# A two-block transformer kernel on one core: idle matmuls, parameter loads, factor rows and the differential maps' scaling

## The chip, the core and the metric

The kernel runs on one core of a Trainium2 chip. The metric is device time in microseconds of one execution. Five engines work beside each other, each on its own list of instructions: TensorE (PE in the profile; its weight loads are PEld), VectorE (DVE), ScalarE (ACT), GpSimd (POOL) and SyncE (SP), which here only issues transfers from memory. They wait for each other by semaphores, which the kernel sets by hand.

## What is computed

Two transformer blocks, one after the other, on 256 tokens of width 1024, all in float32:

```python
def first_block(x, ...):
    h = rmsnorm(x, norm_mix_pre)                    # mixer: q, k, v, forget logits, conv, gates
    m = mixer(h, w_in, b_f, conv_w, w_branch, w_out)
    x = x + rmsnorm(m, norm_mix_post)
    f = swiglu(rmsnorm(x, norm_ffn_pre), w_gate_up, w_down)
    return x + rmsnorm(f, norm_ffn_post)

def second_block(x, mem, ...):
    x = x + 0.5 * swiglu_2(rms_norm(x, norm_ffn1), ffn1_w1, ffn1_w3, ffn1_w2)
    x = x + hybrid_mixer(rms_norm(x, norm_mix), ...)     # retention and differential attention
    x = x + memory_attention(rms_norm(x, norm_mem_q), rms_norm(mem, norm_mem_kv), ...)
    x = x + 0.5 * swiglu_2(rms_norm(x, norm_ffn2), ffn2_w1, ffn2_w3, ffn2_w2)
    return rms_norm(x, norm_out)

def diff_attention(q, k, v, lam):                        # inside hybrid_mixer, 4 heads
    ...
        p = jax.nn.softmax(sc, axis=-1)
        a = p[:, :, 0] - lam * p[:, :, 1]
        return jnp.einsum('bhqk,bkhe->bqhe', a.astype(v.dtype), v)
# and on its output: rms_norm(do, diff_norm) * (1.0 - lam_init)
```

The last line matters here: whatever factor a row of `a` carries is divided out again by the root mean square that follows, but for the `EPS` under the root.

## The kernel before

Every weight matrix is cut into chunks of 1 MB (161 of them, numbered in the order of their use). SP loads a chunk into one of three places of `stage`; ACT rounds it to `w_hi` (`hi(c)`, L1002), DVE takes the difference to `w_lo` (`lo(c)`, L1504), and PE multiplies with both, since a float32 product is made of three products of rounded parts: `three` (L425, L426, L427). A place of the ring is free for SP when `lo_done` has counted the chunk that lay there, and for ACT's next write when PE has counted it in `used`. Each engine's list is written out by hand, so the order in which the calls stand in the code is the order on the engine.

- **Opening.** PE runs 10 idle matmuls on a tile of zeros (L648), transposes the two halves of x as they land (L659), with 6 idle matmuls after the first half and 14 after the second (L662), and then makes the product of chunk Q (0), Q+1, K (2), K+1 (3), the small product of the forget logits, V (4, 5), GB (6, 7) and so on. The first product goes block by block as `act_lo` comes, and for its second half waits for chunk 0's second half.
- **Row factors.** A norm's factor per token is not applied to the activations but to the product's result. DVE puts the factors on a diagonal (`spread`, L1538), PE multiplies it with ones (`factor_rows`, L502), ACT copies the result to `rs` (`rows_out`, L1050), and DVE multiplies results by `rs`.
- **Parameters.** Norm gains and other vectors come by 24 small transfers into `par_rows` on SP's queue (`parameters`, L294); PE transposes them (L675), DVE copies them to `par` (L1688).
- **Feed-forward parts** (three, `FFN[0]` to `FFN[2]`). PE makes the product with the gate weights and then with the up weights (`halves_product`, L578 and L583, 16 + 16 matmuls each), then the second gate product, and then multiplies the first hidden piece with the down weights (`ffn_chunk`, L425 on `bank<-w_hi,ffn_hi`). Before that, DVE and ACT make the hidden piece: gate sum (L1602), `lo`, times `rs` (L1614), silu (L1077), times `rs` (L1618), up sum (L1623), product (L1626), rounding (L1084) and difference `ffn_lo` (L1628). In the first of the three, PE also transposes the memory keys ahead of the first down product and DVE scales them (L1856).
- **Differential attention.** ACT makes the exponentials and their sums, DVE turns the eight maps of a tile into four (`difference`, L1935 and L1937), PE transposes them and multiplies with v, ACT takes squares and the root, DVE scales.

Of the kernel before, what the change touches and what calls it, by code (L numbers as in the profile page):

```python
# [16 lines left out]
ALU = mybir.AluOpType  # L17
# [75 lines left out]
def build(nc, a, out):  # L93
    with ExitStack() as ctx:
# [99 lines left out]
        do_f = small[:, 116:124]  # L194
# [40 lines left out]
        ksq_done, ksum_done, kd_done, kn_done = sem("ksq_done"), sem("ksum_done"), sem("kd_done"), sem("kn_done")  # L235
        dsum_done, dd_done, dn_done = sem("dsum_done"), sem("dd_done"), sem("dn_done")
# [52 lines left out]
        def parameters(engine):  # L289

            engine.wait_ge(zeroed, 1)
# [27 lines left out]
        def _(sp):  # L319
# [58 lines left out]
            sp.dma_start(wf[:, :, :], w_in.rearrange("(k p) n -> p k n", p=P)[:, :, 1536:1544]).then_inc(wf_landed, 16)  # L378
            parameters(sp)
            wholes(K + 1, w_in, 256 * 3, 1)  # L380
# [41 lines left out]
        def _(pe):  # L422
# [148 lines left out]
            def halves_product(banks, place, ready=None, base=0, between=None):  # L571
# [14 lines left out]
                if ready is None:  # L586
                    for m in range(2):
                        if between is not None and m:
                            between()
                        for k in range(KD):  # L590
                            high(m, k)
                        for k in range(KD):
                            mm = low(m, k)
                else:
                    for k in range(KD):
                        if between is not None and k == 2:
                            between()
                        pe.wait_ge(ready, base + k + 1)
                        for m in range(2):
                            high(m, k)  # L600
                        for m in range(2):
                            mm = low(m, k)
                mm.then_inc(used, 1)

            def feed_forward(f, prep, norm, banks_before, extra=None, between=None):
# [3 lines left out]
                halves_product(gate_banks, base % RING, act_lo_done, 8 * prep, between)  # L609
                pe.wait_ge(lo_done, base + 2)  # L610
                for c in banks_before:
                    wait_read(pe, c)
                halves_product(up_banks, (base + 1) % RING, between=lambda: factor_rows(ROWS.index(norm), ACC))
# [39 lines left out]
            for half in range(2):  # L653
# [7 lines left out]
                for _ in range(6 + 8 * half):  # L661
                    pe.matmul(bank[AUX][:, 0:P], idle, idle, start=True, stop=True)  # L662
# [9 lines left out]

            pe.wait_ge(par_landed, 16 * 24)
            pe.wait_ge(rs_done, 1)
            pe.transpose(bank[SUM][:, 0:P], par_rows[:, :], ident).then_inc(par_turned, 1)  # L675
            up(K, act_hi, act_lo)

            up(K + 1, act_hi, act_lo)
            pe.wait_ge(par_ready, 2)
            pe.matmul(bank[SUM][:, 0:2], ones, lam_p, start=True, stop=True).then_inc(lam_done, 1)  # L680
# [6 lines left out]
            tokens(V, act_hi, act_lo)  # L687
            up(GB, act_hi, act_lo)
# [304 lines left out]
        def _(act):  # L993
# [113 lines left out]
            act.activation(diag[:, 0, 0:1], idle[:, 0:1], copy)  # L1107
# [8 lines left out]
            act.wait_ge(zeroed, 6)  # L1116
            warm(ACT.Sqrt)
# [7 lines left out]
            act.wait_ge(wf_landed, 16)  # L1125
            act.activation(wf_hi4, wf4, copy).then_inc(wf_hi_done, 1)
# [4 lines left out]
            act.wait_ge(lam_done, 1)  # L1131
            act.activation(lam_e, bank[SUM][:, 0:2], table_exp).then_inc(lamx_done, 1)
# [7 lines left out]
            scaled_tok(V, 1, v_tok[:, 1, :], factors[N_X0])  # L1140
            act.wait_ge(table_landed, 64)
# [210 lines left out]
            for t in range(2):  # L1352
                head_deviations(t, do_f, dsum_done, dd_done)
# [134 lines left out]
        def _(dve):  # L1488
# [197 lines left out]

            dve.wait_ge(par_turned, 1)
# [5 lines left out]
            lo(4)  # L1693
            scaled(K, k_T[:, 0:2, :], rs)
            lo(5)

            scaled(K + 1, k_T[:, 2:4, :], rs)
# [8 lines left out]
            lo(8)  # L1706
            dve.wait_ge(lamx_done, 1)
# [4 lines left out]
            dve.wait_ge(fln_done, 1)  # L1712
            dve.scalar_tensor_tensor(logf, fz, 0.0, fe, ALU.min, ALU.subtract).then_inc(logf_done, 1)
            scaled(GB, gb_T[:, 0:2, :], rs)
            lo(9)
            scaled(GB + 1, gb_T[:, 2:4, :], rs)
# [212 lines left out]
            def difference(tile, L, nk):  # L1929

                o = inverse_sums(tile)
                odd = prec[:, o + 1:o + 8:2]
                dve.tensor_scalar(odd, odd, lam, None, ALU.mult)
                first = L[:, 0:8:2, 0:nk]
                then(dve.tensor_tensor(first, first, prec[:, o:o + 8:2, None].to_broadcast([P, 4, nk]), ALU.mult))  # L1935
                for h in range(4):
                    ins = dve.scalar_tensor_tensor(L[:, 2 * h, 0:nk], L[:, 2 * h + 1, 0:nk], prec[:, o + 2 * h + 1:o + 2 * h + 2],  # L1937
                                                   L[:, 2 * h, 0:nk], ALU.mult, ALU.add)
                ins.then_inc(p_done, 1)

            difference(2, L0, P)
            difference(3, L1, T)
            lo(111)
# [4 lines left out]
            scaled(RK + 1, rk_T[:, 2:4, :], rs)  # L1948
            for t in range(2):
# [126 lines left out]
            gained(par, G_FFN2, 6, range(2, KD))  # L2076
            lo(129)
            mean_square(N_FFN2)
# [21 lines left out]
        def _(pool):  # L2100
# [6 lines left out]

            pool.memset(par_rows[:, :], 0.0).then_inc(zeroed, 1)
            pool.memset(small[:, :], 0.0).then_inc(zeroed, 1)
# [3 lines left out]
            pool.memset(eps_t[:, :], EPS).then_inc(zeroed, 1)  # L2113
# [48 lines left out]
```

## Time and profile before

| | |
|---|---|
| median of 3 runs | 990.9 us (990.3 to 992.75) |
| profiled execution, its own time | 991.39 us |
| its span in the trace | 989.5 us |
| PE busy | 972.8 us, 98% of the span |
| DVE, ACT busy | 69%, 50% |

The profiled execution has 1.9 us around its span, and lies 0.5 us above the median. Busy time counts an engine's instructions; what an engine waited for is in the view of waits, and the timeline puts both in order of time, with starts in us from the span's start.

### The profile page before, as it was taken

What the parts mean: (1) busy time and instruction counts of PE and PEld (TensorE: products, weight loads), DVE (VectorE), ACT (ScalarE), POOL (GpSimd) and SP (SyncE); (2) the same over time, 40 slices, a digit from 0 to 9 for tenths busy, and PEclk for the clock granted to TensorE, in tenths of its full rate; (3) what the DMA queues carried; (4) which work ended last, traced back from release to release, by engine and by line L of the source; (5) the groups of instructions that cost most, each with busy time, mean ns of one, the idle gap of its engine ahead of it and who ended that gap; (6) DMA issues with size and microseconds to landing.
All of it is one profiled execution on the core that took longest, in us unless ns stands there. A gap on an engine that the chain in (4) does not pass through costs nothing.

```text
span 989.5 us, 14245 instructions
## 1 busy us (share of the span) xinstructions
PE 972.8 (98%) x5708; PEld 858.6 (87%) x5708; DVE 679.8 (69%) x695; ACT 498.5 (50%) x668; POOL 13.9 (1%) x20
## 2 busy tenths in 40 slices
PE   8999999999999999999999999999999999999997
PEld 8899999888888888888888888898988888888885
DVE  4557967766777777867776776576665676777776
ACT  6354654773343434833434346574866554343433
POOL 0000000011000000000000000000000000000000
PEclk9999999999999999999999999999999999999999
DMA  6954473653655556546555553635354445656551
GB/s 197 307 177 150 149 277 128 210 194 128 213 178 204 183 199 213 171 130 210 186 196 185 197 212 128 217 124 170 131 169 149 144 153 170 212 170 212 170 170 43
DMA packets 124358, 176.25 MB, mean 178 GB/s; under 512 B 4042, under 2 KB 98460, under 8 KB 124188
## 3 DMA queue, kind: packets, MB, share of 16 engines
q1 hardware_dynamic: 123596, 173.23, 52.8%
q10 hardware_dynamic: 720, 2.43, 0.7%
q8 instruction: 30, 0.49, 0.2%
q14 instruction: 12, 0.10, 0.0%
HBM read 174.60 MB, written 1.05 MB: 178 GB/s over the span
## 4 chain that ended last, share of the span: by engine, by line
PE 89%; DVE 5%; SPq 2%; issue 2%; ACT 2%; DMA 1%; DVEq 0%; ACTq 0%
PE up_banks L578 12%; PE gate_banks L578 11%; PE bank L425 9%; PE bank L426 9%; PE bank L427 9%; PE up_banks L425 7%; PE up_banks L427 7%; PE up_banks L426 7%; PE up_banks L583 6%; PE gate_banks L583 6%; DVE w_lo L1504 1%; SPq L294 1%; PE bank L512 1%; ACT w_hi L1002 1%; DMA stage<-in_w_in 1%
## 5 line engine op out<-in xcount | busy, mean ns | idle before, releaser
L1510 DVE TENSOR_TENSOR w_lo<-stage,w_hi 128x2048 fp32r<-128x2048 f32 x81 | 185.5, 2290 | 96.5 <-ACT w_hi L1009 96.5
L1504 DVE TENSOR_TENSOR w_lo<-stage,w_hi 128x2048 fp32r<-128x2048 f32 x79 | 181.2, 2297 | 91.4 <-ACT w_hi L1002 91.3
L1002 ACT ACTIVATE w_hi<-stage 128x2048 fp32r<-128x2048 f32 x79 | 150.7, 1911 | 75.5 <-PE up_banks L427 40.5
L1009 ACT ACTIVATE w_hi<-stage 128x2048 fp32r<-128x2048 f32 x81 | 152.6, 1903 | 0.0
L578 PE MATMUL gate_banks<-act_both,w_hi 128*128 128x512 f32 x528 | 135.5, 393 | 0.0
L578 PE MATMUL up_banks<-act_both,w_hi 128*128 128x512 f32 x528 | 131.9, 392 | 0.2 <-DVE w_lo L1504 0.2
L425 PE MATMUL up_banks<-act_both,w_hi 128*128 128x256 f32 x416 | 119.3, 287 | 1.8 <-DVE q_pad L1678 1.2
L426 PE MATMUL up_banks<-act_both,w_hi 128*128 128x256 f32 x416 | 117.8, 283 | 0.0
L427 PE MATMUL up_banks<-act_both,w_lo 128*128 128x256 f32 x416 | 117.7, 283 | 0.0
L578 PEld LDWEIGHTS up_banks<-act_both,w_hi 128*128 128x128 f32 x528 | 96.6, 188 | 18.8 <-DVE w_lo L1504 0.4
L578 PEld LDWEIGHTS gate_banks<-act_both,w_hi 128*128 128x128 f32 x528 | 93.9, 189 | 15.8
L425 PE MATMUL bank<-w_hi,ffn_hi 128*128 128x512 f32 x240 | 94.2, 392 | 3.8 <-issue 3.0
L1084 ACT ACTIVATE ffn_hi<-gate 128x512 fp32r<-128x512 f32 x30 | 18.9, 631 | 154.9 <-DVE gate L1626 154.9
L426 PE MATMUL bank<-w_lo,ffn_hi 128*128 128x512 f32 x240 | 93.8, 391 | 0.0
L427 PE MATMUL bank<-w_hi,ffn_lo 128*128 128x512 f32 x240 | 93.5, 390 | 0.0
L1077 ACT ACTIVATE gate<-gate 128x512 f32<-128x512 f32 x33 | 20.9, 632 | 127.9 <-DVE gate L1614 127.9
L425 PEld LDWEIGHTS up_banks<-act_both,w_hi 128*128 128x128 f32 x416 | 79.8, 192 | 3.2 <-DVE w_lo L1504 2.2
L583 PEld LDWEIGHTS gate_banks<-act_both,w_lo 128*128 128x128 f32 x528 | 74.5, 190 | 6.8
L426 PEld LDWEIGHTS up_banks<-act_both,w_hi 128*128 128x128 f32 x416 | 79.8, 192 | 0.1
L427 PEld LDWEIGHTS up_banks<-act_both,w_lo 128*128 128x128 f32 x416 | 79.8, 192 | 0.0
L583 PEld LDWEIGHTS up_banks<-act_both,w_lo 128*128 128x128 f32 x528 | 72.0, 190 | 5.2
L583 PE MATMUL gate_banks<-act_both,w_lo 128*128 128x256 f32 x528 | 76.4, 282 | 0.0
(337 smaller groups left out, 1492.1 us busy)
## 6 DMA issues: line engine op xcount, KB each, us to landing
stage<-in_ffn_w SPq DMA_DIRECT2D x66, 1024.0 KB, 5.3
stage<-in_w_in SPq DMA_DIRECT2D x33, 1024.0 KB, 5.3
stage<-in_w_gate_up SPq DMA_DIRECT2D x22, 1024.0 KB, 5.2
stage<-in_w_down SPq DMA_DIRECT2D x11, 1024.0 KB, 5.0
stage<-in_w_out SPq DMA_DIRECT2D x8, 1024.0 KB, 4.9
stage<-in_mem_w_kv SPq DMA_DIRECT2D x8, 1024.0 KB, 5.1
stage<-in_w_branch SPq DMA_DIRECT2D x4, 1024.0 KB, 5.2
stage<-in_mem_w_q SPq DMA_DIRECT2D x4, 1024.0 KB, 5.0
```

The lines of the kernel that those rows point to most:

```text
L294: engine.dma_start(par_rows[r:r + n, at:at + cols], src).then_inc(par_landed, 16)
L425: pe.matmul(dst, w, x, start=first, stop=False, skip_group_check=not group)
L426: pe.matmul(dst, w, lo_x, start=False, stop=False, skip_group_check=not group)
L427: return pe.matmul(dst, lo_w, x, start=False, stop=last, skip_group_check=not group)
L578: return pe.matmul(banks[:, m, :], wh[:, k, m * P:m * P + P], act_both[:, k, :, :].rearrange("p s t -> p (s t)"), start=k == 0, stop=False ...
L583: return pe.matmul(banks[:, m, T:2 * T], wl[:, k, m * P:m * P + P], act_both[:, k, 0, :], start=False, stop=k == KD - 1, skip_group_check= ...
L1002: act.activation(w_hi[:, place, :], stage[:, place, :], copy).then_inc(hi_done, 1)
L1009: act.activation(w_hi[:, place, :], stage[:, place, :], copy).then_inc(hi_done, 1)
L1077: act.activation(silu, g_s, ACT.Silu).then_inc(silu_done, 1)
L1084: act.activation(to, h_T, copy).then_inc(ffn_hi_done, 1)
L1504: dve.tensor_tensor(w_lo[:, place, :], stage[:, place, :], w_hi[:, place, :].bitcast(F32), ALU.subtract).then_inc(lo_done, 1)
L1510: dve.tensor_tensor(w_lo[:, place, :], stage[:, place, :], w_hi[:, place, :].bitcast(F32), ALU.subtract).then_inc(lo_done, 1)
```

## The change

- The idle matmuls after the first half of the transposes become 12 instead of 6; those after the second half, ahead of the first product, are gone.
- ACT's first instruction is a square root on a constant instead of a copy; the second warming of the root later on is gone. POOL clears `small` and `eps_t` first.
- SP issues chunk K+1 ahead of the 24 parameter transfers. PE's transposing of the parameters goes from after Q+1 to after K+1, and the small product for lambda to after V; DVE's and ACT's parts follow.
- `factor_rows` of the feed-forward parts stands between the gate and the up product instead of in the middle of the up product.
- In `difference` the maps are no longer multiplied by the inverse of their sums: the even map stays as it is, the odd one is scaled by lambda times the ratio of the sums, and `EPS` in the norm that follows is multiplied by the square of the even sum instead.
- In the last feed-forward part DVE does `lo(129)` between the third and fourth pair of `gained` blocks and not after all of them.

```diff
-            engine.wait_ge(zeroed, 1)
+            engine.wait_ge(zeroed, 3)
...
+            wholes(K + 1, w_in, 256 * 3, 1)
             parameters(sp)
-            wholes(K + 1, w_in, 256 * 3, 1)
...
                     for m in range(2):
-                        if between is not None and m:
-                            between()
...
                 halves_product(gate_banks, base % RING, act_lo_done, 8 * prep, between)
+                factor_rows(ROWS.index(norm), ACC)
                 pe.wait_ge(lo_done, base + 2)
                 for c in banks_before:
                     wait_read(pe, c)
-                halves_product(up_banks, (base + 1) % RING, between=lambda: factor_rows(ROWS.index(norm), ACC))
+                halves_product(up_banks, (base + 1) % RING)
...
-                for _ in range(6 + 8 * half):
+                for _ in range(0 if half else 12):
                     pe.matmul(bank[AUX][:, 0:P], idle, idle, start=True, stop=True)
...
+            up(K, act_hi, act_lo)
+
+            up(K + 1, act_hi, act_lo)
             pe.wait_ge(par_landed, 16 * 24)
             pe.wait_ge(rs_done, 1)
             pe.transpose(bank[SUM][:, 0:P], par_rows[:, :], ident).then_inc(par_turned, 1)
-            up(K, act_hi, act_lo)
-
-            up(K + 1, act_hi, act_lo)
-            pe.wait_ge(par_ready, 2)
-            pe.matmul(bank[SUM][:, 0:2], ones, lam_p, start=True, stop=True).then_inc(lam_done, 1)
...
             tokens(V, act_hi, act_lo)
+            pe.wait_ge(par_ready, 2)
+            pe.matmul(bank[SUM][:, 0:2], ones, lam_p, start=True, stop=True).then_inc(lam_done, 1)
...
-            act.activation(diag[:, 0, 0:1], idle[:, 0:1], copy)
+            act.wait_ge(zeroed, 2)
+            warm(ACT.Sqrt)
...
             act.activation(w_hi[:, 0, second], stage[:, 0, second], copy).then_inc(hi_done, 1)
-            act.wait_ge(zeroed, 6)
-            warm(ACT.Sqrt)
             hi(1)
...
             for t in range(2):
-                head_deviations(t, do_f, dsum_done, dd_done)
+                act.wait_ge(dmean_done, t + 1)
+                s = do_f[:, 4 * t:4 * t + 4]
+                act.activation(s, s, ACT.Sqrt).then_inc(dd_done, 1)
...
-                o = inverse_sums(tile)
-                odd = prec[:, o + 1:o + 8:2]
-                dve.tensor_scalar(odd, odd, lam, None, ALU.mult)
-                first = L[:, 0:8:2, 0:nk]
-                then(dve.tensor_tensor(first, first, prec[:, o:o + 8:2, None].to_broadcast([P, 4, nk]), ALU.mult))
+
+                o = 8 * (tile % 2)
+                dve.wait_ge(exp_done, tile + 1)
+                even, odd = psum_[:, o:o + 8:2], prec[:, o + 1:o + 8:2]
+                then(dve.reciprocal(odd, psum_[:, o + 1:o + 8:2]))
+                then(dve.scalar_tensor_tensor(odd, even, lam, odd, ALU.mult, ALU.mult))
...
+            for t in range(2):
+                even = psum_[:, 8 * t:8 * t + 8:2]
+                then(dve.scalar_tensor_tensor(do_eps[:, 4 * t:4 * t + 4], even, EPS, even, ALU.mult, ALU.mult))
...
+            for t in range(2):
+                dve.wait_ge(dsum_done, t + 1)
+                s = slice(4 * t, 4 * t + 4)
+                dve.scalar_tensor_tensor(do_f[:, s], do_f[:, s], 1.0 / P, do_eps[:, s], ALU.mult, ALU.add).then_inc(dmean_done, 1)
...
-            gained(par, G_FFN2, 6, range(2, KD))
+            gained(par, G_FFN2, 6, range(2, 4))
             lo(129)
+            gained(par, G_FFN2, 6, range(4, KD))
```

The order on SP at the opening, before: the transfers of chunk 1, of the constants, of chunk 2, of `wf` and of the parameters (24 in 17 rows, the first and the last shown), then chunk 3, chunks 4 and 5.

```order
L332 DMA stage<-in_w_in 128x8x256
L376 DMA const<-in_consts 128x768
L332 DMA stage<-in_w_in 128x8x256
L378 DMA wf<-in_w_in 128x8x8
L294 DMA par_rows<-in_norm_mix_pre 8x128
...
L294 DMA par_rows<-in_b_f 1x8 x4
L332 DMA stage<-in_w_in 128x8x256
L339 DMA stage<-in_w_in 128x4x512 x2
```

And of the change (lines of the changed kernel are one higher here):

```order
L377 DMA const<-in_consts 128x768
L333 DMA stage<-in_w_in 128x8x256
L379 DMA wf<-in_w_in 128x8x8
L333 DMA stage<-in_w_in 128x8x256
L295 DMA par_rows<-in_norm_mix_pre 8x128
...
L295 DMA par_rows<-in_b_f 1x8 x4
L340 DMA stage<-in_w_in 128x4x512 x2
```

The third chunk-sized transfer has moved ahead of all parameter transfers; nothing else on this queue has moved.

The order on DVE where the last feed-forward part begins, before: the last residual add, the low parts of the activations (L1517), chunk 129's low part (L1504), the sum of squares, the inverse and the diagonal.

```order
L1545 TENSOR_TENSOR x_n<-bank,x_n 128x512
L1517 SCALAR_TENSOR_TENSOR act_both<-bank,par,act_both 128x256 x6
L1504 TENSOR_TENSOR w_lo<-stage,w_hi 128x2048
L1524 TENSOR_TENSOR norms<-norms 128x2
L1529 RECIPROCAL norms<-norms 128x2
L1538 TENSOR_SCALAR diag<-const,norms 128x128 x2
```

And of the change:

```order
L1547 TENSOR_TENSOR x_n<-bank,x_n 128x512
L1519 SCALAR_TENSOR_TENSOR act_both<-bank,par,act_both 128x256 x2
L1506 TENSOR_TENSOR w_lo<-stage,w_hi 128x2048
L1519 SCALAR_TENSOR_TENSOR act_both<-bank,par,act_both 128x256 x4
L1526 TENSOR_TENSOR norms<-norms 128x2
L1531 RECIPROCAL norms<-norms 128x2
L1540 TENSOR_SCALAR diag<-const,norms 128x128 x2
```

The chunk's low part now stands ahead of the last four activation blocks.

The order on PE at the same place, before: the end of the gate product, the up product in two halves with the factor rows (L502) between them, and the second gate product.

```order
L583 MATMUL gate_banks<-act_both,w_lo 128x256 x2
L578 MATMUL up_banks<-act_both,w_hi 128x512 x8
L583 MATMUL up_banks<-act_both,w_lo 128x256 x8
L502 MATMUL bank<-diag,const 128x128 x2
L578 MATMUL up_banks<-act_both,w_hi 128x512 x8
L583 MATMUL up_banks<-act_both,w_lo 128x256 x8
```

And of the change:

```order
L584 MATMUL gate_banks<-act_both,w_lo 128x256 x2
L503 MATMUL bank<-diag,const 128x128 x2
L579 MATMUL up_banks<-act_both,w_hi 128x512 x8
L584 MATMUL up_banks<-act_both,w_lo 128x256 x8
L579 MATMUL up_banks<-act_both,w_hi 128x512 x8
L584 MATMUL up_banks<-act_both,w_lo 128x256 x8
```

The two matmuls with the diagonal have moved ahead by half of the up product, and now stand directly behind the gate product. It is the same in all three feed-forward parts.

## Rows read from the trace of the kernel before

**Rows 1.** The page: busy time of each engine.

```profile
PE 972.8 (98%) x5708; PEld 858.6 (87%) x5708; DVE 679.8 (69%) x695; ACT 498.5 (50%) x668; POOL 13.9 (1%) x20
```

**Rows 2.** Waits of PE, whole span: us in total, times, longest.

```profile
PE bank L425 <- issue: 3.0, 2, 1.5
...
PE up_banks L425 <- DVE q_pad L1678: 1.2, 1, 1.2
...
PE bank L425 <- DVE k_mem L1856: 0.6, 1, 0.6
PE up_banks L425 <- DVE gate L1569: 0.6, 1, 0.6
```

**Rows 3.** Timeline of the opening: start, duration, engine, line, tile, [idle before].

```profile
1.04 3.94 PE L648 MATMUL gate_banks<-L 128*128 128x128 f32 x20 [1.04 <-DVE L L1654]
...
6.79 1.50 PE L662 MATMUL gate_banks<-L 128*128 128x128 f32 x12
...
9.87 1.09 PE L659 MATMUL bank<-const,x_n 128*128 128x128 f32 x8 [1.57 <-DMA x_n<-in_x]
...
10.80 3.29 PE L662 MATMUL gate_banks<-L 128*128 128x128 f32 x28
...
13.11 1.23 DVE L1659 TENSOR_TENSOR w_lo<-stage,w_hi 128x1024 fp32r<-128x1024 f32 x1
...
13.85 0.36 PE L425 MATMUL up_banks<-act_both,w_hi 128*128 128x256 f32 x1
...
14.50 1.90 ACT L1002 ACTIVATE w_hi<-stage 128x2048 fp32r<-128x2048 f32 x1
...
16.43 2.29 DVE L1504 TENSOR_TENSOR w_lo<-stage,w_hi 128x2048 fp32r<-128x2048 f32 x1 [2.10 <-ACT w_hi L1002]
```

**Rows 4.** DMA issues at 3.91 us, chunk 1: count, size, us from issue to landing.

```profile
stage<-in_w_in SPq DMA_DIRECT2D x1, 1024.0 KB, 10.4
```

**Rows 5.** Windows of 13.8 to 19.6: length, each engine's busy time (instructions), granted clock.

```profile
13.80:19.60 5.80, 5.80 (x51) 5.80 (x50) 3.16 (x4) 5.56 (x13) 0.00 (x0) 1.00 0.69 189
```

**Rows 6.** Chain of waits in 0 to 60: start, us, what.

```profile
11.98 3.54 SPq L294
...
22.68 5.35 DMA stage<-in_w_in
28.05 1.92 ACT w_hi L1002
30.07 2.29 DVE w_lo L1504
...
33.11 0.36 PE up_banks L425
```

**Rows 7.** Timeline of the second feed-forward part's beginning.

```profile
415.86 0.49 DVE L1538 TENSOR_SCALAR diag<-const,norms 128x128 f32<-128x128 f32 x2
...
422.89 0.61 PE L502 MATMUL bank<-diag,const 128*128 128x128 f32 x4
...
423.53 0.39 ACT L1050 ACTIVATE rs<-bank 128x256 f32<-128x256 f32 x1 [4.59 <-PE bank L502]
```

**Rows 8.** Chain of waits there, 409 to 434: the up product's start and the wait.

```profile
420.28 1.82 PE up_banks L578 x8
...
431.88 1.51 issue
```

**Rows 9.** Timeline of the third feed-forward part's beginning.

```profile
798.59 1.66 DVE L1517 SCALAR_TENSOR_TENSOR act_both<-bank,par,act_both 128x256 fp32r<-128x256 f32 x4 [1.22 <-ACT act_both L1017]
...
799.37 0.63 PE L578 MATMUL gate_banks<-act_both,w_hi 128*128 128x512 f32 x2
...
803.09 0.48 DVE L1538 TENSOR_SCALAR diag<-const,norms 128x128 f32<-128x128 f32 x2
...
806.08 0.37 ACT L1050 ACTIVATE rs<-bank 128x256 f32<-128x256 f32 x1
```

**Rows 10.** The line of DVE's scaling of the even maps.

```profile
L1935 DVE TENSOR_TENSOR L<-L,small x2: 685/952/1220, 663.2 to 665.5; 128x512 f32<-128x512 f32 x1, 128x1024 f32<-128x1024 f32 x1
```

More of the change, by code:

```diff
@@ L193, in build @@
         diff_f, diffk_f = small[:, 84:100], small[:, 100:116]
-        do_f = small[:, 116:124]
+        do_f, do_eps = small[:, 116:124], small[:, 140:148]
         ro_mean, ro_f = small[:, 124:132], small[:, 132:140]
@@ L235, in build @@
         ksq_done, ksum_done, kd_done, kn_done = sem("ksq_done"), sem("ksum_done"), sem("kd_done"), sem("kn_done")
+        dmean_done = sem("dmean_done")
         dsum_done, dd_done, dn_done = sem("dsum_done"), sem("dd_done"), sem("dn_done")
@@ L1125, in _ @@
             act.wait_ge(wf_landed, 16)
+            act.wait_ge(zeroed, 6)
             act.activation(wf_hi4, wf4, copy).then_inc(wf_hi_done, 1)
@@ L1130, in _ @@
             hi(7)
-            act.wait_ge(lam_done, 1)
-            act.activation(lam_e, bank[SUM][:, 0:2], table_exp).then_inc(lamx_done, 1)
             act.wait_ge(r_done, N_X0 + 1)
@@ L1140, in _ @@
             scaled_tok(V, 1, v_tok[:, 1, :], factors[N_X0])
+            act.wait_ge(lam_done, 1)
+            act.activation(lam_e, bank[SUM][:, 0:2], table_exp).then_inc(lamx_done, 1)
             act.wait_ge(table_landed, 64)
@@ L1685, in _ @@
             dve.tensor_tensor(wf_lo4, wf4, wf_hi4.bitcast(F32), ALU.subtract).then_inc(wf_lo_done, 1)
+            lo(4)
+            scaled(K, k_T[:, 0:2, :], rs)
+            lo(5)
+            scaled(K + 1, k_T[:, 2:4, :], rs)
             dve.wait_ge(par_turned, 1)
@@ L1692, in _ @@
                               ).then_inc(par_ready, 1)
[L1693 to L1697, printed above, removed]
             lo(6)
@@ L1706, in _ @@
             lo(8)
-            dve.wait_ge(lamx_done, 1)
-            then(dve.tensor_tensor(lam, lam_e[:, 1:2], lam_e[:, 0:1], ALU.subtract))
-            then(dve.tensor_scalar(lam, lam, -LAM_INIT, None, ALU.add))
-            then(dve.tensor_scalar(par[:, DIFN:DIFN + 1], par[:, DIFN:DIFN + 1], 1.0 - LAM_INIT, None, ALU.mult))
             dve.wait_ge(fln_done, 1)
@@ L1716, in _ @@
             scaled(GB + 1, gb_T[:, 2:4, :], rs)
+            dve.wait_ge(lamx_done, 1)
+            then(dve.tensor_tensor(lam, lam_e[:, 1:2], lam_e[:, 0:1], ALU.subtract))
+            then(dve.tensor_scalar(lam, lam, -LAM_INIT, None, ALU.add))
+            then(dve.tensor_scalar(par[:, DIFN:DIFN + 1], par[:, DIFN:DIFN + 1], 1.0 - LAM_INIT, None, ALU.mult))
             lo(10)
@@ L2106, in then @@
                 pool.wait_ge(pool_step, steps[0])
+            pool.memset(small[:, :], 0.0).then_inc(zeroed, 1)
+            pool.memset(eps_t[:, :], EPS).then_inc(zeroed, 1)
             pool.memset(par_rows[:, :], 0.0).then_inc(zeroed, 1)
-            pool.memset(small[:, :], 0.0).then_inc(zeroed, 1)
             pool.memset(wf_hi.bitcast(F32), 0.0).then_inc(zeroed, 1)
@@ L2112, in _ @@
             pool.memset(z_T[:, :, 0:2], 0.0).then_inc(zeroed, 1)
-            pool.memset(eps_t[:, :], EPS).then_inc(zeroed, 1)
             for j in range(2):
```

## The prediction

> **What bounds the kernel now.** I read the page first: PE is busy 98% of the span [rows 1], so TensorE's list is the bound and only two things count: work taken from it, and its waits. So the second view is that of PE's waits [rows 2]. There are few. Two of 1.5 us stand before the first down product of the second and third feed-forward part (the view calls them "issue"), one of 0.6 us in the first part, where PE waits for the scaled memory keys. 1.2 us falls in the opening, on a read of the query result, and 0.6 us in differential attention, on DVE's read of RQ+1. The change touches each of these places. The third view is the timeline of the opening, since 20 idle matmuls stand there which do no work but hold PE; the fourth is the chain of waits, which says what is late in each place. DVE and ACT matter only where PE waits for them.
>
> A listed wait counts from the modelled end of the last matmul. In the opening product 51 matmuls start in 5.80 us [rows 5], one in 0.12 us, though one lasts 0.28 to 0.36 [rows 3]. So a wait that goes gives back some 0.16 us more than is listed.
>
> **The opening, idle matmuls.** Each idle matmul is two instructions: 28 of them in 3.29 us [rows 3], 0.117 us each. The second group starts at 10.80 and the first product at 13.85, behind it. Without the group PE could start the product at about 10.97. The first group grows from 12 to 24 instructions: from 6.79 it would end at 6.79 + 24 x 0.117 = 9.6, before the second half of x lands and its transposes start at 9.87. It fills a wait of 1.57 us that is there anyway, and costs nothing. If it ran over, it would delay everything by what it runs over.
>
> What does the earlier start bring? The first product needs 48 x 0.12 = 5.8 us. Its second half waits for the low part of chunk 0's second half, which ends at 13.11 + 1.23 = 14.34 [rows 3]; the half then takes 2.9, so the product ends at 17.3. Before it ended at 13.85 + 5.8 = 19.6. Up to here that is 2.3 us. But the next product needs chunk 1. Its high part starts at 14.50 before, behind the warming of the root, which leaves this place. Without it ACT would be free at 13.1. But chunk 1 is issued at 3.91 and lands 10.4 us later [rows 4], at 14.3. So the high part moves from 14.50 to about 14.35 only, the low part from 16.43 to 16.3, and it ends at 18.6. Q+1 starts at 18.6 and not at 19.6: **1.0 us**. The bounds are 0 (PE finds another thing late) and 2.3 (chunk 1 lands earlier, since a landing is not the same in each execution).
>
> **The opening, parameter loads.** In the chain SP issues parameters from 11.98 to 22.68; then comes chunk 3, lands 5.35 us later, is rounded (1.92) and subtracted (2.29), the query is scaled, and PE starts K+1 at 33.11 [rows 6] after its listed wait of 1.2 us. With the change chunk 3 is issued when chunk 0's low part frees the ring, at 14.4. It queues behind chunk 2 and wf and lands, by an estimate, at 22 (two transfers of 1 MB after 14.3, at some 2.7 to 5.35 us for each). High part by 24.3, behind chunk 2's; low part by 26.6. PE wants K+1 only after Q+1 and K: 18.6 + 6.1 + 5.8 = 30.5. The wait is gone with 4 us to spare: 1.2 + 0.2 = **1.4 us**. What is late next is the V pair, which now stands behind the parameters: issued by 25 at the latest (14.9 and the same 10.7 us that the parameters take in the chain), landed by 31 and 34, low part of the first by 36. PE wants it after K+1 and the forget product, at 39.4. The parameters are wanted at 36.3, 11 us after their issue. Lambda's product and its scalars stand behind other work that has slack of many us. All of this costs nothing. If the V pair were 4 us later than I count, its wait would eat the gain us for us.
>
> **Factor rows.** In the second part the diagonal is done at 415.86 + 0.49 = 416.35 [rows 7], 4 us before the gate product's end at 420.28 [rows 8]. PE reaches the factor rows at 422.89 in the middle of the up product, ACT copies rs at 423.53 after an idle time of 4.59, and then its chunk, DVE's low part, the scaling, silu and the rest follow one behind the other. With the rows ahead of the up product, rs comes at about 420.9, 2.6 us earlier. The wait of 1.51 at 431.88 is shorter than that, so it goes: 1.5 + 0.16, **1.7 us**. The low bound is 0, if the up sum were what is late: it has to follow the up product, which ends no earlier, but it stood behind silu, so I take the full wait. In the first part the same shift frees DVE for the memory keys. Its 0.6 us goes, until PE's own transposes end: **0.7 us**, low bound 0.
>
> In the third part the diagonal is done only at 803.57 [rows 9], later than the gate product's end (a bit over 802), so the moved factor rows would meet a wait of some 1.3 us. The moved `lo(129)` answers to that. DVE sits idle 1.22 us before the last four blocks at 798.59. The low part (2.3 us) fills this time, from 797.4 to 799.7, and the blocks then take 1.66, to 801.3 instead of 800.25. PE reaches block 4 at 799.37 before and at about 800.15 then, 0.8 later. The sum of squares, which stood behind `lo(129)`, comes 1.0 earlier, and so the diagonal by about 0.8, at 802.8, when PE ends the gate product at 803.1: no wait. ACT copies rs at 806.08 behind its chunk and a table load, which all hang on the diagonal's chain, and comes 0.85 earlier, not 2.6. So the down product starts 0.85 earlier: **0.85 us**, bounded by -0.5 (the rows do wait for the diagonal) and 1.7.
>
> **Differential maps.** The two multiplies that go are 0.685 and 1.220 us [rows 10]; two smaller ones on 128x4 are added before `lo(111)`, some 0.2 each by the small rows around, and one is waited for. DVE gains 1.4 us, more than PE's 0.6 us behind it: **0.7 us**. The low bound is 0, if another wait stands right behind. The later small steps (sum plus epsilon, root) add 0.4 us to a chain with 4 us of slack before its transposes.
>
> **The sum:** 1.0 + 1.4 + 1.7 + 0.7 + 0.85 + 0.7 = 6.35. The profiled execution took 991.4, so 985.0; it lies 0.5 above the median of the runs, and 990.9 - 6.35 is 984.5. I say 984.6.
>
> **The clock, and a rule that speaks against the change.** In the opening the same idle instruction takes 3.94 / 20 = 0.197 us at first and 0.117 later [rows 3], with a granted clock of 1.00, the level of 2.4 GHz, in the stretch of the first product [rows 5]; so the engine starts slow, near the lower level of 1.2 GHz, and has risen by 6.79. It kept the high level over the idle time of 1.57 us before 9.87. The change leaves less idle time there, and two new short ones (0.5 at 13.9, 1.3 at 17.3). The Trainium skill, in TensorE: Matmul & The Clock Gate, "Part 1: The HAM clock gate", says that the throttled level is the default and that only activity releases it. By that, taking activity away could bring the low level back, and every matmul of the opening would take twice its time; by the trace, it does not, and the sum stands.
>
> **Rivals.**
> - *The opening gives nothing, or the waits move on.* Speaks for it: chunk 1 lands at 14.3, chunk 3 and V are only estimated. Then 6.35 - 2.4 = 4.0, or 986.9. If a feed-forward wait stays too, 988. Against it: the 4 us of slack at each. Chance 0.20.
> - *More than forecast.* Chunk 1 lands early, and the third part loses its whole wait: 6.35 + 1.3 + 0.85 = 8.5, or 982.4. Chance 0.08.
> - *It does not do what it says.* PE's waits are refilled, since the transfers and ACT set the pace after all: 990 to 991. Against it stands PE's 98%. Chance 0.07.
> - *Slower: the clock falls in the opening.* A product of 48 matmuls at the low level costs 5.8 us more. The gain without the idle matmuls' 1.0 is 5.4, so from one product at the low level on there is no gain, and from one and a half on (8.7 - 5.4 = 3.3 us) the kernel is slower by what can be told. If it fell for Q, Q+1 and K: 17.4 - 5.4 = 12, or 1002.9. Against it: 1.57 us of idle did not lower it. Chance 0.03.
> - The forecast, 983 to 986.5: 0.62.
>
> **The numbers.** 0.3% is 3.0 us, about what a measurement of this kernel can tell from no change. Faster by more than that means under 987.9: the forecast, "more", and nearly all of the first rival, 0.88. Same 0.09, slower 0.03. The lower ends of the terms give 3.3 or so (1.4 + 1.2 + 0.7) and the upper ends 8.5 to 9, so the range is 982.1 to 987.6.
>
> **What would show it.** The first product starts at 11.0, halts at 13.9 and ends at 17.3; Q+1 starts at 18.6, K+1 by 30.6 without a wait. PE's waits lose both "issue" rows of 1.5 or keep one of under 0.5, and the rows on k_mem, q_pad and DVE's gate. The factor rows of the third part start at 803 less the shift so far. DVE's line for the even maps is gone, and the span is 983.2. It would be wrong if the instructions of 0.197 us went on past 11, if PE waited at V or at the diagonal of the third part, or if a new wait stood at the down products.

## The result, and the profile after

| | before | after |
|---|---|---|
| median of the runs on the same chip | 990.96 us (990.3 to 992.75, 4 runs) | 983.85 us (983.41 to 984.09, 4 runs) |
| profiled execution, its own time | 991.39 us | 984.04 us |
| its span | 989.5 us | 982.2 us |

The ratio is 0.9927, with a 95% interval of 0.9915 to 0.9939. The kernel is 7.1 us faster, and the time forecast, 984.6 us, is 0.75 us too high. The page of the changed kernel, answering to [rows 1], shows PE with 16 instructions and 2.3 us less of work:

```profile
PE 970.5 (99%) x5692; PEld 856.6 (87%) x5692; DVE 678.4 (69%) x697; ACT 497.7 (51%) x666; POOL 16.7 (2%) x20
```

The remaining 5 us of the span are waits that went. The view of PE's waits (whole span; us in total, times, longest), answering to [rows 2]:

```profile
PE up_banks L426 <- DVE w_lo L1506: 1.4, 1, 1.4
PE gate_banks L648 <- DVE L L1656: 1.0, 1, 1.0
PE up_banks L426 <- DVE w_lo L1661: 0.6, 1, 0.6
PE gate_banks L579 <- DVE act_both L1519: 0.5, 1, 0.5
PE bank L659 <- DMA x_n<-in_x: 0.5, 1, 0.5
PE bank L955 <- ACT L L1432: 0.2, 1, 0.2
...
```

Both waits of 1.5 us ("issue") are gone, and so are those on `q_pad`, `k_mem` and `gate`. Three are new: 0.6 and 1.4 us in the opening, on low parts of chunks 0 and 1, where the idle matmuls stood, and 0.5 at the third feed-forward part.

**Where the time came from.** To divide the 7.3 us of the span by place, I compared when DVE starts the low part of the same chunk in both traces. The shift, before less after, behind each changed place:

| behind | shift, us | this place gave | forecast |
|---|---|---|---|
| the opening | 2.59 | 2.59 | 2.4 |
| 1st feed-forward part | 3.42 | 0.83 | 0.7 |
| 2nd feed-forward part | 5.18 | 1.76 | 1.7 |
| differential attention | 5.93 | 0.75 | 0.7 |
| 3rd feed-forward part | 7.23 | 1.30 | 0.85 |

The opening in the timeline of the changed kernel (start, duration, engine, line, tile, idle before), answering to [rows 3]:

```profile
6.06 2.84 PE L662 MATMUL gate_banks<-L 128*128 128x128 f32 x24
9.35 1.09 PE L659 MATMUL bank<-const,x_n 128*128 128x128 f32 x8 [0.45 <-DMA x_n<-in_x]
12.59 1.22 DVE L1661 TENSOR_TENSOR w_lo<-stage,w_hi 128x1024 fp32r<-128x1024 f32 x1
13.85 1.31 SPq L333 DMA_DIRECT2D stage<-in_w_in  x1
14.05 1.91 ACT L1002 ACTIVATE w_hi<-stage 128x2048 fp32r<-128x2048 f32 x1 [1.49 <-DMA stage<-in_w_in]
15.99 2.29 DVE L1506 TENSOR_TENSOR w_lo<-stage,w_hi 128x2048 fp32r<-128x2048 f32 x1 [2.17 <-ACT w_hi L1002]
18.43 0.36 PE L426 MATMUL up_banks<-act_both,w_hi 128*128 128x256 f32 x1 [1.36 <-DVE w_lo L1506]
24.31 2.29 DVE L1506 TENSOR_TENSOR w_lo<-stage,w_hi 128x2048 fp32r<-128x2048 f32 x1 [0.64 <-ACT w_hi L1002]
31.96 2.29 DVE L1506 TENSOR_TENSOR w_lo<-stage,w_hi 128x2048 fp32r<-128x2048 f32 x1 [4.42 <-ACT w_hi L1002]
```

The 24 idle instructions end before the second half of x lands, as forecast. (That holds for this execution; three of the experiments' traces, in the last section, show them running past it.) Q+1 starts at 18.43 (forecast 18.6) behind chunk 1's low part. Chunk 3 is issued at 13.85, and its low part ends at 26.60, 3.9 us before K+1 wants it; that of the first V chunk ends at 34.25, and V starts at 39.19. The prediction counted on 4 us of slack for each, and no wait stands at either.

The chain of waits (start, us, what) names what holds the opening now. It is not PE, but chunk 1, from its issue at 3.83 on:

```profile
3.83 10.19 DMA stage<-in_w_in
...
18.43 0.36 PE up_banks L426
```

In the second feed-forward part, the timeline answers to [rows 7]. ACT's copy stands 1.81 us idle and not 4.59, and everything behind it comes 6.2 us earlier in the trace, of which 3.4 were there already:

```profile
417.34 0.39 ACT L1050 ACTIVATE rs<-bank 128x256 f32<-128x256 f32 x1 [1.81 <-PE bank L503]
```

The low part that the down product needs starts at 426.42, and the product itself at 428.46 without a wait.

In the third part, the timeline answers to [rows 9]:

```profile
791.36 2.28 DVE L1506 TENSOR_TENSOR w_lo<-stage,w_hi 128x2048 fp32r<-128x2048 f32 x1
793.55 1.66 DVE L1519 SCALAR_TENSOR_TENSOR act_both<-bank,par,act_both 128x256 fp32r<-128x256 f32 x4
794.09 0.73 PE L579 MATMUL gate_banks<-act_both,w_hi 128*128 128x512 f32 x2 [0.47 <-DVE act_both L1519]
795.12 0.15 DVE L1526 TENSOR_TENSOR norms<-norms 128x2 f32<-128x2 f32 x1
795.84 0.48 DVE L1540 TENSOR_SCALAR diag<-const,norms 128x128 f32<-128x128 f32 x2
796.98 0.61 PE L503 MATMUL bank<-diag,const 128*128 128x128 f32 x4
798.84 0.37 ACT L1050 ACTIVATE rs<-bank 128x256 f32<-128x256 f32 x1
```

The diagonal is done at 796.32 and PE comes to it at 796.98, so the factor rows meet no wait. With the shift of 5.93 added, these rows stand on the clock of [rows 9]: the diagonal starts at 801.77 instead of 803.09, and `rs` at 804.77 instead of 806.08. Both are 1.3 us earlier.

### The profile page after: what moved, and what is told of

Its sections match the earlier page's. It is cut to its first block, busy times and chain, and to the rows that moved or that the text cites. A ratio compares the mean times of both kernels' runs of the same rounds, so it can differ in the third digit from the quotient of the medians.

```text
span 982.2 us, 14216 instructions
## 1 busy us (share of the span) xinstructions
PE 970.5 (99%) x5692; PEld 856.6 (87%) x5692; DVE 678.4 (69%) x697; ACT 497.7 (51%) x666; POOL 16.7 (2%) x20
## 4 chain that ended last, share of the span: by engine, by line
PE 94%; DVE 2%; ACT 1%; DMA 1%; issue 1%; SPq 0%; DVEq 0%; ACTq 0%
PE up_banks L579 12%; PE gate_banks L579 12%; PE bank L426 9%; PE bank L427 9%; PE bank L428 9%; PE up_banks L426 9%; PE up_banks L428 8%; PE up_banks L427 8%; PE up_banks L584 6%; PE gate_banks L584 6%; DMA stage<-in_w_in 1%; PE bank L513 1%; DVE w_lo L1506 1%; PE bank L530 1%; PE bank L721 0%
## 5 line engine op out<-in xcount | busy, mean ns | idle before, releaser
L1506 DVE TENSOR_TENSOR w_lo<-stage,w_hi 128x2048 fp32r<-128x2048 f32 x79 | 180.9, 2294 | 84.7 <-ACT w_hi L1002 84.5
```

The lines of the kernel that those rows point to most:

```text
L1506: dve.tensor_tensor(w_lo[:, place, :], stage[:, place, :], w_hi[:, place, :].bitcast(F32), ALU.subtract).then_inc(lo_done, 1)
```

## The experiments

Each ratio is to the kernel before on the same chip. The changed kernel was measured beside a kernel before of 990.96 us; the four runs on the opening beside one of 990.84, the next four beside 990.66, the last two (`v_split`, below) beside 990.63. So a median that is compared with the 983.85 us of the changed kernel can be off by 0.3 us from that alone. "Loses" means against the changed kernel, by the shift of the same instruction in the traces. Between two changed places such a shift keeps its value to 0.05 us at most chunks. The opening itself comes differently in each execution: chunk 1, issued at 3.6 to 3.9 us, landed between 13.3 and 14.3 us in the twelve traces.

**Opening, idle matmuls alone.** The changed kernel with the 14 idle matmuls back ahead of the first product:

```diff
-                for _ in range(0 if half else 12):
+                for _ in range(14 if half else 12):
```

> The changed kernel with the second group of 14 idle matmuls put back ahead of the first product. My theory (the idle matmuls held PE, but chunk 1 sets the second product): the second product starts 0.8 to 1.1 us later than in the changed kernel and everything behind it too, so 984.8 us. Rival (the gain of the opening is all the earlier chunk 3): no difference, 983.9. Rival (the idle matmuls keep the clock up): faster than the changed kernel.

Measured 984.76 us (984.28 to 984.94), ratio 0.9938 (0.9921 to 0.9956). The trace loses 0.9 us from chunk 7's low part to the end. PE's waits, from the longest:

```profile
PE gate_banks L648 <- DVE L L1656: 1.0, 1, 1.0
PE gate_banks L579 <- DVE act_both L1519: 0.5, 1, 0.5
PE bank L955 <- ACT L L1432: 0.2, 1, 0.2
...
```

The rows on L1506 and L1661 of the changed kernel are not there: the idle matmuls fill exactly that time and 0.9 us more. The other way round, the kernel before with the second group taken away (and the first made 12):

```diff
-                for _ in range(6 + 8 * half):
+                for _ in range(0 if half else 12):
```

> The kernel before with only the idle groups changed (12 and 0 instead of 6 and 14). By my theory that K+1 waits for chunk 3 anyway this gives nothing: 990.9, and PE's wait before K+1 grows by what is gained before it. Rival (each edit is worth its term): 1.0 us faster, 989.9.

Measured 990.65 us (989.4 to 992.29, 10 runs), ratio 1.0002 (0.9992 to 1.0012). The same edit that is worth 0.9 us in the changed kernel is worth nothing here by the medians, which alone could hide 1 us (the interval). Its waits of PE say why it is nothing:

```profile
PE up_banks L425 <- DVE q_pad L1678: 2.1, 1, 2.1
PE up_banks L425 <- DVE w_lo L1504: 1.4, 1, 1.4
```

Q+1 starts as early as in the changed kernel, but K+1 waits for the query that stands behind chunk 3 on DVE. That wait was 1.2 [rows 2] and is 2.1 now. PE stood at K 1.3 us earlier than in the kernel before, and K+1 starts at 32.62, 0.5 us earlier; that this 0.5 is no gain either is shown next.

**Opening, parameter loads.** The changed kernel with chunk 3 issued behind the parameters again:

```diff
-            wholes(K + 1, w_in, 256 * 3, 1)
             parameters(sp)
+            wholes(K + 1, w_in, 256 * 3, 1)
```

> The changed kernel with the 24 parameter transfers issued ahead of chunk 3 again. If the two edits of the opening add up, as my sum had them (1.0 and 1.4), this loses 1.4 us, 985.3. My theory now is that they don't: chunk 3's chain is set by SP's queue, so K+1 starts at 33 us whatever PE does before, and the whole 2.6 us of the opening is lost: 986.4.

Measured 985.72 us (985.13 to 987.41), ratio 0.9951 (0.9934 to 0.9969); the trace loses 2.2 us. The median, 1.9 above the changed kernel's, lies between the two expectations (1.4 and 2.6 lost); the place decides. K+1 starts at 32.63, as in the experiment before, whatever PE did ahead of it. Again PE's waits:

```profile
PE up_banks L426 <- DVE q_pad L1680: 2.2, 1, 2.2
PE up_banks L426 <- DVE w_lo L1506: 1.2, 1, 1.2
```

These make a table of four. Against the profiled execution of before, the shift behind the opening is 0 with neither edit, 0.48 and 0.36 in the two kernels with the idle edit alone in effect, 1.71 with the parameters' place alone, and 2.59 with both. The first is not quite the right zero: in that execution of before, SP itself was late. It issues chunk 3 at 22.68 [rows 6], and at 22.22 and 22.25 in the two kernels with the idle edit alone, whose transfers stand in the same order. The chain of waits with the parameters first:

```profile
22.25 5.30 DMA stage<-in_w_in
```

So some 0.45 of each shift is that late queue, which leaves 0, 0, 1.3 and 2.2. The parameters' place is worth 1.3 us if PE comes late and 2.2 if it comes early; the idle matmuls are worth nothing without it, and 0.9 with it.

**Factor rows.** The changed kernel with them back in the middle of the up product, `lo(129)` left early:

```diff
...
-                factor_rows(ROWS.index(norm), ACC)
...
-                halves_product(up_banks, (base + 1) % RING)
+                halves_product(up_banks, (base + 1) % RING, between=lambda: factor_rows(ROWS.index(norm), ACC))
```

> The changed kernel with the factor rows of the feed-forward parts back in the middle of the up product; everything else as changed. My theory (the rows' place sets the chain to the first down product): the shifts of 0.8 (first part), 1.8 (second) and 1.3 (third) are all lost, 3.9 us in sum, 987.7. Rival (in the third part the earlier lo(129) alone makes the gain): 2.6 lost, 986.4.

Measured 987.91 us (987.41 to 988.04, 8 runs), ratio 0.9973 (0.9962 to 0.9984): 4.1 us of 7.1 are lost. In the traces it loses 0.8 in the first part, 1.7 in the second and 1.55 in the third (3.83 us at the last chunk, less 2.28 ahead of that part). Its waits of PE and the chain in the second part:

```profile
PE bank L426 <- issue: 3.0, 2, 1.5
...
PE bank L426 <- DVE k_mem L1859: 0.6, 1, 0.6
```

```profile
429.03 1.51 issue
```

All three waits of before are back, in the form that they had. That the third part loses 1.55 and not 1.3 shows what the early `lo(129)` does when it stands alone: it stops PE for 0.5 us at the fourth block, and block 4 comes 0.65 us later. Of this PE gets back 0.35, since its listed wait of 0.2 for chunk 129's low part ahead of the up product goes. The rest stays: 0.24 us lost against the kernel before.

**`lo(129)`.** The changed kernel with this low part behind all blocks:

```diff
-            gained(par, G_FFN2, 6, range(2, 4))
+            gained(par, G_FFN2, 6, range(2, KD))
             lo(129)
-            gained(par, G_FFN2, 6, range(4, KD))
```

> The changed kernel with lo(129) behind all blocks again. My theory: the diagonal of the third part comes 1.3 us later, PE waits some 1.2 us at the factor rows, and the down product starts 1.3 us later than in the changed kernel: 985.1. Rival (PE's wait at block 4 goes and pays for it): no difference, 983.9.

Measured 984.89 us (984.66 to 985.04), ratio 0.9943 (0.9926 to 0.9959). The third part gives nothing. The timeline there:

```profile
796.86 0.48 DVE L1540 TENSOR_SCALAR diag<-const,norms 128x128 f32<-128x128 f32 x2
797.40 0.71 PE L503 MATMUL bank<-diag,const 128*128 128x128 f32 x4 [1.30 <-DVE diag L1540]
799.85 0.37 ACT L1050 ACTIVATE rs<-bank 128x256 f32<-128x256 f32 x1
```

PE waits 1.30 us for the diagonal, the wait that the prediction named for this case. In the third part neither edit is worth anything by itself (0 for the rows' place, -0.24 for the early `lo(129)`); the two together are worth 1.3.

**Differential maps.** The changed kernel with the maps scaled as before, and `EPS` plain:

```diff
-                then(dve.reciprocal(odd, psum_[:, o + 1:o + 8:2]))
-                then(dve.scalar_tensor_tensor(odd, even, lam, odd, ALU.mult, ALU.mult))
+                o = inverse_sums(tile)
+                odd = prec[:, o + 1:o + 8:2]
+                dve.tensor_scalar(odd, odd, lam, None, ALU.mult)
+                first = L[:, 0:8:2, 0:nk]
+                then(dve.tensor_tensor(first, first, prec[:, o:o + 8:2, None].to_broadcast([P, 4, nk]), ALU.mult))
...
```

> The changed kernel with the differential maps scaled by the inverse sums again. My theory: 0.75 us slower, 984.6, with a wait of 0.6 us on DVE's scaling of RQ+1 back. Rival (the small steps added behind cost as much as the two multiplies saved): no difference.

Measured 984.25 us (983.92 to 984.34), ratio 0.9936 (0.992 to 0.9953). The trace loses 0.75 us between the places ahead of and behind the attention, and this row is back among PE's waits, 0.6 listed:

```profile
PE up_banks L426 <- DVE gate L1569: 0.6, 1, 0.6
```

The median is 0.4 above the changed kernel's; with each counted against the kernel before on its own chip it is 0.7 (gains of 6.4 and 7.1). That the profiled executions are alike in time (984.19 and 984.04) is the opening's variation: chunk 1 landed 0.7 us earlier in this one, which puts its trace 0.69 us ahead up to the attention.

**The first group of idle matmuls** back to 6, the second still gone (`range(0 if half else 6)`):

> The changed kernel with 6 idle matmuls after the first half of x instead of 12. My theory: they fill a wait for x and nothing else: no difference, 983.9, with PE's wait before the second transposes longer by 1.4 us. Rival (the longer idle time lets the clock fall): the transposes and the first product take twice their time for a stretch, 1 us or more slower.

Measured 983.52 us (982.94 to 983.71), ratio 0.9928 (0.9911 to 0.9944). PE waits 0.9 us for x's second half instead of 0.5. I had expected 1.4 more, not 0.4: in this execution the transposes of the first half began 0.7 us later, and the second half landed 0.2 earlier. The trace is 0.3 us ahead from chunk 7's low part to the end, as much as chunk 1 landed earlier (13.7 against 14.0); the growth of this group to 12 is worth nothing.

**No idle matmul at all,** neither the 10 ahead of the transposes nor the 12 between them:

```diff
-            for _ in range(10):
-                pe.matmul(bank[AUX][:, 0:P], idle, idle, start=True, stop=True)
...
-                for _ in range(0 if half else 12):
+                for _ in range(0):
```

> The changed kernel with no idle matmul at all, neither the first 10 nor the 12. My theory: the first transposes and the first product then start at the lower level of the clock, and the first product runs at 0.24 us a matmul until it rises; the wait for chunk 1 (1.4 us) covers that much of it, so 1 to 5 us slower than the changed kernel. Rival (idle matmuls do nothing at all): 983.9.

Measured 983.82 us (983.06 to 984.53), ratio 0.9932 (0.9914 to 0.995). My theory, 1 us slower or more, fell by the median. But two of the four runs are at 984.26 and 984.53, above every run of the changed kernel, and the profiled one (983.39) is of the fast two. The timeline of PE shows the slow stretch that the theory spoke of:

```profile
4.99 1.97 PE L657 MATMUL bank<-const,x_n 128*128 128x128 f32 x8 [0.44 <-DMA x_n<-in_x]
8.97 1.97 PE L657 MATMUL bank<-const,x_n 128*128 128x128 f32 x8 [2.01 <-DMA x_n<-in_x]
...
10.95 0.41 PE L427 MATMUL up_banks<-act_both,w_hi 128*128 128x256 f32 x1
11.16 0.41 PE L428 MATMUL up_banks<-act_both,w_lo 128*128 128x256 f32 x1
...
13.30 0.37 PE L426 MATMUL up_banks<-act_both,w_hi 128*128 128x256 f32 x1
...
13.63 0.28 PE L428 MATMUL up_banks<-act_both,w_lo 128*128 128x256 f32 x1
```

Matmuls of 256 columns start every 0.213 us until 13.3 and every 0.12 from there: 256 columns in 0.213 us are one column a cycle at 1.2 GHz, the lower level. The transposes, 1.97 us for eight, take 1.09 in the changed kernel. So 12 matmuls lose 1.1 us and the transposes of the second half 0.9. In the changed kernel the first product has two waits around it, 0.6 us for chunk 0's second half and 1.4 for chunk 1, and these take the whole loss: here no wait is left, and Q+1 starts at 17.79, just behind chunk 1's low part (15.35 + 2.29 = 17.64, this chunk having come 0.6 earlier than in the changed kernel's trace).

**A version that takes the remaining wait.** Chunk 1's rounding and low part are done in two halves, as chunk 0's are, and Q+1 starts after the first. The row factors of the first norm, which stand inside Q+1, move from its third to its sixth block; the lines below are ACT's and DVE's part:

```diff
...
-            hi(1)
+            act.wait_ge(landed[1], 16)
+            act.activation(w_hi[:, 1, first], stage[:, 1, first], copy).then_inc(half1_hi_done, 1)
+            act.activation(w_hi[:, 1, second], stage[:, 1, second], copy).then_inc(hi_done, 1)
...
-            lo(1)
+            half_lo(slice(0, CH // 2), half1_hi_done, half1_lo_done, 1)
+            half_lo(slice(CH // 2, CH), hi_done, lo_done, 1)
...
```

> The changed kernel, with chunk 1's rounding on ScalarE and its low part on VectorE done in two halves (as chunk 0's are), and the product Q+1 starting after the first half. Theory: in the opening of the changed kernel TensorE waits 1.36 us for chunk 1's low part, which stands 4.2 us of work behind the landing; with halves the first half of the low part is ready at about 17.1, so Q+1 starts there and that wait goes. The product K behind it then waits for the query result and chunk 2's low part until about 23.8, so that of 1.36 some 0.7 us is kept: 983.1 us against 983.85, at most 982.5. Rival: the wait moves on whole (to chunk 2's low part or to the query's read), the gain is 0 and the time 983.8. The place where it shows: VectorE's low part of chunk 4 starts 0.7 us earlier (theory) or at the same time (rival).

Measured 983.23 us (983.11 to 983.41, 5 runs), ratio 0.9928 (0.9914 to 0.9941). By the times it can't be told from the changed kernel: the ratios are 0.9928 and 0.9927, the gains on each one's own chip 7.4 and 7.1 us. The place that I had named, chunk 4's low part, starts at 31.87 against 31.96, which by the expectation's words is the rival's sign. It was badly chosen: ACT rounds this chunk only when it lands, in both kernels.

```profile
29.92 1.92 ACT L1005 ACTIVATE w_hi<-stage 128x2048 fp32r<-128x2048 f32 x1 [5.35 <-DMA stage<-in_w_in]
```

PE shows more. Q+1 starts at 17.53 instead of 18.43, and everything on PE and, from chunk 7 on, nearly every low part comes 0.92 us earlier to the end. Chunk 1 landed 0.2 us earlier in this execution, so 0.7 is what the halves give, in one trace. PE's waits in the opening and at the third feed-forward part:

```profile
PE up_banks L427 <- DVE w_lo L1666: 0.6, 1, 0.6
PE gate_banks L580 <- DVE act_both L1524: 0.5, 1, 0.5
```

The row of 1.4 us is gone. Q+1 follows the first product at once, so that what is left is the wait of 0.6 us inside that product, for chunk 0's second half. K starts at 23.72 without a wait, where I had expected it to be held until 23.8.

**The same without any idle matmul:**

> The kernel v_split without any idle matmul (neither the 10 ahead of the transposes nor the 12 between them). The changed kernel without any idle matmul took the same time as with them, its first product running at 0.213 us a matmul until 13.3 us and at 0.12 from there. Theory: that cost nothing because a wait stood behind it, for chunk 0's second half and then for chunk 1's low part; with that second wait halved the slow stretch is covered less, so this kernel is 0.5 to 1.2 us slower than v_split. Rival: chunk 1's landing still decides, the idle matmuls are worth nothing here either, and both take the same time within 0.3 us.

Measured 983.22 us (983.08 to 984.17, 5 runs). The medians are those of the rival: no difference. But the profiled execution is the one of 984.17, and its timeline of PE says this:

```profile
14.81 0.41 PE L429 MATMUL up_banks<-act_both,w_lo 128*128 128x256 f32 x1
...
15.20 0.28 PE L428 MATMUL up_banks<-act_both,w_hi 128*128 128x256 f32 x1
```

Here the low level lasts to 15.0 and not to 13.3, the product finds no wait to hide it in, and the trace is 1.08 us behind that of `v_split`. So the mechanism is shown in one execution, and the idle matmuls would be worth 1.1 us in it. How often it comes is open (the two slower runs without idle matmuls above may be the same): three of the five runs are at 983.1 to 983.2, and with the idle matmuls the runs spread by 0.3 us instead of 1.1.

## Why the prediction was right

It was right in time and in mechanism, place by place, but for one assumption in the sum: that the two terms of the opening stand each by itself.

- **Idle matmuls, 1.0 us.** Q+1 at 18.43 against 18.6, bound by chunk 1's landing, as worked out; undoing it loses 0.9. The step treated the term as free-standing, and there it was incomplete: alone it is worth 0 (ratio 1.0002), since K+1 waits for a transfer whose time does not depend on PE. The prediction's sum holds only because the parameters are moved too. Its rival "the waits move on" is right for this edit alone. The warming of the root, which left ACT's list ahead of chunk 1's rounding, was put back in no run; by the rows of before it held that rounding by 0.2 us at most (landed at 14.3, started at 14.50).
- **Parameter loads, 1.4 us.** 1.3 with the idle matmuls in place. Undoing it in the changed kernel loses 2.2, its own 1.3 and the idle matmuls' 0.9, for the same reason. Chunk 3 landed 7.6 us behind its issue, at 21.4 (22 by the estimate, whose 2.7 us for a transfer no row shows), and its low part ended at 26.60 against 26.6; that of V at 34.25 against "by 36".
- **The opening's 2.59 us** holds some variation too. In the profiled execution of before, x's second half landed later than in the other traces, [rows 3] 9.87 against 9.35 in the changed kernel, and chunk 1 at 14.3 against 14.0. The medians give 7.1 - 4.6 (the other four places) = 2.5, the table of four 2.2; the forecast of 2.4 lies between. That it does is in part luck, since it was read from an execution with a queue some 0.45 us late.
- **Factor rows, second part 1.7 us:** 1.76. **First part 0.7:** 0.83. In both the whole listed wait goes and some 0.25 more, where the second paragraph of the prediction has 0.16. The rest is that the first matmul behind such a wait keeps the next one off for 0.31 us instead of 0.23 (815.92 and 816.23 in the kernel before).
- **Third part, 0.85 us:** 1.30. This is the mis-sized term, 0.45 of the 0.75 us by which the time was too high. The mechanism held: `lo(129)` fills the idle time, block 4 comes 0.65 later (0.8 forecast), the rows meet no wait. The error is in the step "the sum of squares comes 1.0 earlier, and so the diagonal by about 0.8". I had added up durations, but each DVE row starts some 0.08 us before the end that is printed for the one before it, so my 801.3 for the sum of squares was 801.05, 1.32 earlier; and between it and the diagonal nothing in the rows takes back 0.2, so that discount had no ground. The whole chain up to `rs` moved by the 1.22 us of idle time that was filled, and 0.1 more.
- **Differential maps, 0.7 us:** 0.75 by the traces of the changed kernel and of the experiment.
- **The clock.** The 0.197 us of the prediction is a mean over both levels: in that trace the idle instructions start every 0.213 us until 4.0 us and every 0.112 from there. The rival "the clock falls" did not come: the first product runs at 0.12 us a matmul in the changed kernel. Its trace agrees with the part of the Trainium skill's rule that was cited, TensorE: Matmul & The Clock Gate, "Part 1: The HAM clock gate", in so far as the engine starts at the low level and stays there longer where work is taken away (until 13.3 and 15.0 without idle matmuls, 6.9 at the latest with them). What was wrong in the rival is its price. I had 5.8 us a product and nothing to hide it. At 0.213 us instead of 0.12 a whole product of 48 would cost 4.5 us more, and without any idle matmul only a part of one was at that level: the trace shows 1.1 us in the product and 0.9 in the transposes, and the waits beside them hid it all.

## What to carry to other kernels

When two waits stand one behind the other on a path, taking away the first alone is worth nothing if the second is for a transfer with a time of its own: work out the gain of each edit with and without the other, and look for the fixed event that comes last. When work moves into idle time on an engine, shift the starts of the rows behind it as a block rather than adding up printed durations. A moved consumer needs its producer moved with it: the factor rows and `lo(129)` give 1.3 us together, and 0 and -0.24 each by itself. And a place that is to tell two theories apart must wait for the engine in question: chunk 4's low part waited for a landing.

## What was unexpected of the hardware

- Warming matmuls were worth nothing by the medians as long as the low level's loss, some 2 us, lay ahead of a transfer that came later anyway (983.82 us against 983.85); two of the four runs without them were 0.2 and 0.4 us above the highest with them.
- The time at which the level rises is not the same in executions that begin with the same instructions. Without idle matmuls it was 13.3 and 15.0, the transposes having begun at 4.99 and 8.97, and at 5.91 and 9.37. With the 20 idle instructions from 1.04 us on, it was 4.0 in the kernel before and 6.9 in `v_split`, where the transposes of the first half still take 1.70 us instead of 1.09:

```profile
5.81 1.70 PE L660 MATMUL bank<-const,x_n 128*128 128x128 f32 x8
7.35 2.84 PE L663 MATMUL gate_banks<-L 128*128 128x128 f32 x24
10.03 1.04 PE L660 MATMUL bank<-const,x_n 128*128 128x128 f32 x8
```

- So the 24 idle instructions can be too many. Here they end only when the transposes at 10.03 begin, and x's second half had landed at 9.4; it is the same in the experiments on the factor rows and on `lo(129)` (9.93 and 9.97, landed at 9.2). The prediction names this case as one that delays everything; it delayed nothing behind chunk 1's low part, whose wait was 0.6 and 0.5 us in those two instead of 1.4. In `v_split`, where that wait is gone, it probably does cost something: the low part of chunk 0's second half, for which the first product waits, starts at 13.22 there and at 12.59 in the changed kernel. No run tested it.
- The view of windows does not show it. For the kernel without idle matmuls its granted clock (the number behind POOL's) is 1.00 in the stretch in which each matmul took 0.41 us:

```profile
11.00:13.30 2.30, 2.30 (x13) 2.30 (x13) 2.23 (x5) 1.76 (x3) 0.00 (x0) 1.00 1.08 368
```

So at the start of this kernel the level is read from the distance between two matmuls, not from that column. The prediction, which took the 1.00 as proof of the high level for the first product, was right by its other ground, the 0.12 us between matmuls.
